# Dilated attention of the sample batches: each key scored once, its multiplicity in the bias, new keys in spare columns

## The reference, cut to what matters

```python
DIL_CONFIGS = ((128, 1), (512, 4), (2048, 16))

def _dilated_sample(q, kv_all, n_buf, slopes):
    outs, lses = [], []
    for win, dil in DIL_CONFIGS:
        j = jnp.arange(win // dil + 1)
        idx = n_buf + jnp.arange(Tn)[:, None] - j[None] * dil
        g = kv_all[:, jnp.maximum(idx, 0)]
        s = jnp.einsum('bqhd,bqjhd->bhqj', q, g[:, :, :, 0]).astype(jnp.float32) * SCALE
        s = s - slopes[:, None, None] * (j * dil).astype(jnp.float32)
        p, lse = _masked_softmax(s, idx >= 0)
        ...
    return _combine_dilations(outs, lses)     # weights: softmax over the three lses
```

## Time and profile before

| what | value |
|---|---|
| median of three runs | 2346.24 us |
| span of the profiled execution (no other time is given for it) | 2350.6 us |
| PE busy | 2262.0 us, 96% of the span |
| DVE, POOL, ACT busy | 891.3, 647.0, 566.5 us |
| mean granted TensorE clock | 0.988 |
| bytes moved | 448.21 MB |
| one sample batch | 39.2 us, 16 of them |

### The profile page before, as it was taken

One profiled execution on the slowest core, in us unless ns is written; L12 is line 12 of the kernel. 1 busy time (PEld: TensorE's weight loads), 2 busy tenths in 40 slices (PEclk: granted clock), 3 DMA queues, 4 the chain that ended last, 5 costly groups with the idle time before them and its releaser, 6 DMA issues.

```text
span 2350.6 us, 43764 instructions
## 1 busy us (share of the span) xinstructions
PE 2262.0 (96%) x13712; PEld 1618.1 (69%) x13712; DVE 891.3 (38%) x2374; ACT 566.5 (24%) x1356; POOL 647.0 (28%) x719
## 2 busy tenths in 40 slices
PE   7999999999999999999999999999999999999998
PEld 4545567676766777777745556667676677777776
DVE  2003764333353222336510147434344522233374
ACT  2111651112122422220111046311111133221202
POOL 0001760101043343344100047410102424343340
PEclk8999999999999999999999999999999999999999
DMA  9643017888864454455375320387888535444441
GB/s 348 218 165 94 6 55 269 294 295 288 301 251 149 167 185 167 167 194 193 115 268 197 134 63 0 133 301 283 306 286 299 211 117 205 179 180 172 167 167 41
DMA packets 128819, 448.21 MB, mean 191 GB/s; under 512 B 17953, under 2 KB 89890, under 8 KB 107554
## 3 DMA queue, kind: packets, MB, share of 16 engines
q1 hardware_dynamic: 118768, 416.45, 48.6%
q10 hardware_dynamic: 9906, 29.98, 3.7%
HBM read 435.76 MB, written 152.57 MB: 250 GB/s over the span
## 4 chain that ended last, share of the span: by engine, by line
PE 89%; issue 4%; DVE 4%; DMA 1%; POOL 1%; ACT 1%; DVEq 0%; SPq 0%; POOLq 0%; ACTq 0%
PE bank L1067 39%; PE bank L1150 14%; PE bank L1363 10%; PE bank L1431 3%; PE bank L1539 3%; PE bank L1298 2%; PE bank L1330 2%; PE bank L1310 2%; PE bank L1163 1%; PE bank L1485 1%; PE bank L1564 1%; POOL zone L919 1%; PE bank L1048 1%; PE bank L1511 1%; PE bank L1541 1%
## 5 line engine op out<-in xcount | busy, mean ns | idle before, releaser
L1067 PE MATMUL bank<-zone,ring 128*128 128x288 f32 x1664 | 426.3, 408 | 9.2 <-DVE zone L1704 6.6
L1067 PEld LDWEIGHTS bank<-zone,ring 128*128 128x128 f32 x1664 | 316.1, 191 | 103.0 <-DVE zone L1704 12.0
L1067 PE MATMUL bank<-zone,w 128*128 128x288 f32 x1408 | 353.5, 406 | 0.0
L1150 PE MATMUL bank<-ring,hT 128*128 128x512 f32 (+2 forms) x800 | 334.5, 572 | 6.8 <-DMA ring<-in_w_in 5.0
L1067 PEld LDWEIGHTS bank<-zone,w 128*128 128x128 f32 x1408 | 267.5, 190 | 73.9
L1150 PEld LDWEIGHTS bank<-ring,hT 128*128 128x128 f32 (+1 forms) x800 | 149.0, 191 | 161.4 <-issue 150.2
L873 POOL TENSOR_TENSOR w<-ring 128x512 f32<-128x512 f32 x72 | 95.6, 1328 | 555.9 <-PE bank L1067 309.4
L1363 PE MATMUL bank<-ring,w 128*128 128x128 f32 x2048 | 242.5, 277 | 0.0
L1363 PEld LDWEIGHTS bank<-ring,w 128*128 128x128 f32 x2048 | 233.0, 192 | 4.1 <-issue 3.8
L611 ACT COPY zone<-bank 128x288 f32<-128x288 f32 x72 | 28.6, 398 | 569.5 <-PE bank L1067 569.5
L986 POOL TENSOR_TENSOR zone<-constants,stat 128x1024 f32<-128x1024 f32 x16 | 30.3, 1896 | 457.2 <-DVE stat L2063 457.2
(11 more groups left out here) (256 smaller groups left out, 2791.2 us busy)
## 6 DMA issues: line engine op xcount, KB each, us to landing
out_dil_s<-in_state_kv_dil SPq DMA_DIRECT2D x48, 2720.0 KB, 12.1
ring<-in_w_units SPq DMA_DIRECT2D x72, 1024.0 KB, 4.8
zone<-in_dilated_v SPq DMA_DIRECT2D x16, 3072.0 KB, 12.7
ring<-in_cache_kv_cmp SPq DMA_DIRECT2D x256, 128.0 KB, 2.2
ring<-in_cache_kv_sel SPq DMA_DIRECT2D x256, 128.0 KB, 6.1
ring<-in_w_in SPq DMA_DIRECT2D x10, 2048.0 KB, 8.6
zone<-in_dilated_k SPq DMA_DIRECT2D x16, 1280.0 KB, 6.0
zone<-in_dilated_k SPq DMA_DIRECT2D x16, 1024.0 KB, 8.1
```

The costliest lines, as they stand in the source:

```text
L1067: last = mm(dst[:, 0:HALF], lhs[:, k, :], rhs(k), start=first and k == 0, stop=(k == 3), skip_group_check=True)
L1150: last = mm(dst, hT[:, k, t * P:t * P + ROWS[t]], ring[:, n % 2, k * CH:k * CH + width], start=start and k == 0, stop=stop and k == KT - 1)
```

## The change

The dilated keys are held once. A key that several of the three sets hold is scored once, and the logarithm of its count is added to its bias. The keys are: the last 128 (tile "last"); the near tiles, now without those 128, which leaves 96 keys in each; and the far tiles, now without the last 512, which leaves 96 keys in each. The 8 new keys of the batch itself sit in 8 free columns of each near tile, which is then 104 wide. The scores of a batch take 128 + 104 + 96 = 328 columns of a bank, not 448. The tile count stays 13.

POOL writes the new keys into the near tiles for each batch once SP's load is there (`new_keys`), and PE waits for POOL in place of the load. The new values come by a small DMA from the output `dil_s`, to which the projections have stored them; the values are loaded by four DMAs and no longer by two. The matmuls L1465 and L1541 are gone, as are DVE's pair for the new keys and the closing minimum. ACT copies the transposed probabilities in three pieces of 128, 104 and 96 rows, and PE waits for each piece before the first tile that uses it.

```diff
+NEAR, FAR = 96, 96
+K_NEAR = NEAR + NS
+AT_NEAR, AT_FAR = P, P + K_NEAR
+KEYS_D = AT_FAR + FAR
...
                 def load_dilated_k(b):
-                    sp.dma_start(kda, of_batch("dilated_k", b)[:, 0:ND_A, :]).then_inc(kda_ld.sem, 16)
-                    sp.dma_start(kdb, of_batch("dilated_k", b)[:, ND_A:ND_A + 4, :]).then_inc(kdb_ld.sem, 16)
+                    keys = i["dilated_k"][L, ds(b, 1)].rearrange("o q p f -> (o q p) f")
+                    sp.dma_start(kda, keys[:, 0:KA]).then_inc(kda_ld.sem, 16)
+                    sp.dma_start(kdb, keys[:, KA:KA + KB]).then_inc(kdb_ld.sem, 16)
...
-                load_dilated_v(0, 0, ND_TILES - 1)
+                load_dilated_v(0)
...
+                    sp.dma_start(vd[:, 0, :], i["dilated_v_last"][L, ds(b, 1)].rearrange("o q p f -> (o q p) f")).then_inc(
+                        vd_ld.sem, 16)
+                    sp.dma_start(vd[0:NEAR, 1:ND_TILES - 1, :], of_batch("dilated_v", b)[:, 0:ND_TILES - 2, :]).then_inc(
+                        vd_ld.sem, 16)
+                    new = o["dil_s"][L, ds(b, 1), PAST - NS:PAST, CH:2 * CH].rearrange("o q r f -> (o q r) f")
+                    sp.dma_start(vd[NEAR:K_NEAR, 1:5, :], new.unsqueeze(1).to_broadcast([NS, 4, CH])).then_inc(vd_ld.sem, 16)
...
-                    copy(ptd[:, 0:3, :].rearrange("p e r -> p (e r)"), B[:, 0:384])
-                    copy(ptd[0:64, 3, :], B[0:64, 384:512]).then_inc(ptk_act.sem, 1)
+                    for e, R in enumerate((P, K_NEAR, FAR)):
+                        copy(ptd[0:R, e, :], B[0:R, e * P:(e + 1) * P]).then_inc(ptk_act.sem, 1)
...
+                def new_keys(it, b):
+                    pool.wait_ge(s_pad.sem, s_pad.at(it, 1))
+                    pool.wait_ge(kda_ld.sem, kda_ld.at(it, 1))
+                    pool.sem_inc(waits_taken_pool, 1)
+                    nc.gpsimd.tensor_copy(kd_near[:, :, :, NEAR:K_NEAR],
+                                          knb[:, :, ds(b * NS, NS)].unsqueeze(1).to_broadcast([P, 4, 4, NS])).then_inc(
+                                              kd_new.sem, 1)
...
-                    pe.wait_ge(kda_ld.sem, kda_ld.at(it, 1))
+                    pe.wait_ge(kd_new.sem, kd_new.at(it, 1))
...
-                    for p in range(4):
-                        mm(S[:, 384:448], strips[:, 0, p * P:(p + 1) * P], knb[:, p, :], start=False, stop=(p == 3),
-                           skip_group_check=True)
...
-                    mm(bank[7][:], ptd[0:64, 3, :], vsm[:, 256:768], start=False, stop=True,
-                       skip_group_check=True).then_inc(od_full.sem, 1)
...
-                    negated(s_d[:, 0:384], B[:, 0:384], const["b_dil"][:], sm[:, 24:25])
-                    step(new_scores(s_d[:, 384:448], B[:, 384:448], const["nb_newd"][:, new], sm[:, 25:26]))
-                    V.tensor_reduce(stat[:, 26:27], sm[:, 24:26], X, ALU.min).then_inc(td_used.sem, 1)
+                    negated(s_d, B[:, 0:KEYS_D], const["b_dil"][:], stat[:, 26:27]).then_inc(td_used.sem, 1)
```

More of the change, by code:

```diff
@@ L275, in build @@
         s_win = part(m + 1216, 576, rows=high)
-        s_d = part(m + 2048, 448)
+        s_d = part(m + 2048, KEYS_D)
         d_own = part(m + 1792, 512)
@@ L280, in build @@
         ptw = part(stg_at + 1024, 5, 64)
-        ptd = part(stg_at + 1344, 4, P)
+        ptd = part(stg_at + 1344, 3, P)
         gb, gm = part(m + 2496, 192, rows=low), part(m + 2048, 192)
@@ L890, in _ @@
                     kind, t = z_kind(n)
-                    if kind not in ("cs", "wg", "vb"):
+                    if kind not in ("cs", "wg", "vb") or n == NZ - 1:
                         continue
@@ L1520, in batch @@
                     B = bank[TD_BANK[TD_PTD]]
-                    for e in range(4):
-                        R = 64 if e == 3 else P
-                        last = tr(B[0:R, e * P:(e + 1) * P], s_d[:, e * P:e * P + R], ident[:])
+                    for e, (a, z) in enumerate(((0, AT_NEAR), (AT_NEAR, AT_FAR), (AT_FAR, KEYS_D))):
+                        last = tr(B[0:z - a, e * P:(e + 1) * P], s_d[:, a:z], ident[:])
                     last.then_inc(td_full.sem, 1)
-                    pe.wait_ge(vd_ld.sem, vd_ld.at(it, 2))
-                    pe.wait_ge(ptk_act.sem, ptk_act.at(it, 3))
-                    pe.sem_inc(waits_taken_pe, 1)
+                    pe.wait_ge(vd_ld.sem, vd_ld.at(it, 4))
                     for j in range(ND_TILES):
+                        if j in (0, 1, ND_A):
+                            pe.wait_ge(ptk_act.sem, ptk_act.at(it, 3 + (0, 1, ND_A).index(j)))
+                            pe.sem_inc(waits_taken_pe, 1)
                         if j == ND_A:
@@ L2206, in laid_out, with turned @@
     put["state_kv_dil"] = dil.reshape(DEPTH, NB, PAST, D)
-    by4 = dil[:, :, PAST - 4 * P:].reshape(DEPTH, NB, P, 4, 2, 8, HD)
-    by16 = dil.reshape(DEPTH, NB, P, 16, 2, 8, HD)[:, :, :, 0:8]
-    tiles = np.concatenate([dil[:, :, PAST - P:, None], by4, by16], 3)
-    put["dilated_v"] = tiles[..., 1, :, :].reshape(DEPTH, NB, P, ND_TILES, CH)
-    put["dilated_k"] = tiles[..., 0, :, :].reshape(DEPTH, NB, P, ND_TILES, 4, 2, HD).transpose(
-        0, 1, 5, 6, 3, 4, 2).reshape(DEPTH, NB, P, ND_TILES, CH)
+    last = dil[:, :, PAST - P:]
+    near = dil[:, :, PAST - WIN:PAST - P].reshape(DEPTH, NB, NEAR, 4, 2, 8, HD)
+    far = dil.reshape(DEPTH, NB, P, 16, 2, 8, HD)[:, :, 0:FAR, 0:8]
+    put["dilated_v_last"] = last[..., 1, :, :].reshape(DEPTH, NB, P, CH)
+    put["dilated_v"] = np.concatenate([near, far], 3)[..., 1, :, :].reshape(DEPTH, NB, NEAR, ND_TILES - 1, CH)
+    def turned(rows, room):
+        k = rows[..., 0, :, :].reshape(DEPTH, NB, rows.shape[2], -1, 4, 2, HD).transpose(0, 1, 5, 6, 3, 4, 2)
+        k = np.pad(k, [(0, 0)] * 6 + [(0, room - rows.shape[2])])
+        return k.reshape(DEPTH, NB, P, -1)
+    put["dilated_k"] = np.concatenate([turned(last[:, :, :, None], P), turned(near, K_NEAR), turned(far, FAR)], -1)
     return {n: np.ascontiguousarray(v) for n, v in put.items()}
```

72 lines of the change are left out of this document (39 added, 33 removed).

## The result

| | before | after |
|---|---|---|
| median (lowest to highest) | 2346.10 us (2341.94 to 2347.63) | 2378.67 us (2367.63 to 2382.45) |
| profiled span | 2350.6 us | 2380.6 us |
| PE busy | 2262.0 us | 2237.0 us |
| mean granted TensorE clock | 0.988 | 0.977 |
| one sample batch | 39.24 us | 41.93 us (mean of 12) |

The change makes the kernel slower: the ratio is 1.0133, 95% interval 1.0104 to 1.0163. The forecast was 2315 us, range 2303 to 2330. It was wrong, in sign too. The profiled execution of the changed kernel (2382.45 us) is the slowest of its four, 4 us above their median.

What follows compares the result with a forecast made beforehand. TensorE, 89% of the chain, was taken to bound the kernel. Terms 0.31 + 0 + 0.22 + 0.49 + 0.97 = 1.99 us a batch, 31.8 over 16, taken as 31, gave 2315 us; own range 2309 to 2321, with A and B 2303 to 2330.

Steps and rivals of the forecast that it cites:

- Narrower tiles: PE's near and far score matmuls: classes 0.16 and 0.22 us shorter; kept 0.31 early and 0.22 late a batch.
- rival A: Score matmul rounds keep 0.11 us because weight loads set them; 1.46 us a batch saved, 2323 us; chance 0.13.
- the floor of 0.10: Score matmuls: by the skill's 25 ns minimum between starts, a round of four could not fall under 0.10 us.
- L1465 gone: Removed matmul before L1475: its 1.04 us becomes waiting for DVE's `gs`, 1.2 us idle in all; kept 0.
- rival D: The clock falls in the new 1.2 us idle time before L1475; 2342 us, no change; chance 0.04.
- C: Rival: all removed PE work counts, 3.19 us a batch, needing `gs` a microsecond earlier; 2295 us; chance 0.06.
- Transposes and copies: Dilated probabilities before L1539: one transpose fewer, and PE starts after ACT's first, 128-column copy; kept 0.49 us a batch.
- L1541 gone: Removed matmul before L1548, 1.05 us: kept 0.97 us a batch, with 0.08 of new idle time.
- rival E: Value matmuls on tiles of 96 and 104 rows lose their overlap; 101 us slower, 2447 us; chance 0.05.
- POOL's new keys: POOL's copy of new keys: hidden, except in a layer's first batch, where 0.4 plus a 0.2 us hop offsets a shorter load.
- the last sentence of the parts: SP's value DMAs, 4 for 2 with 21% fewer bytes: issues covered by its wait for selected outputs, so no time added.
- Rival B: SP sets the pace through late compression pages; PE keeps about 1.0 us a batch, 2330 us; chance 0.07.

Runs made afterwards that it cites:

- e7: e3 with SP issuing the value loads behind the selection's loads and ScalarE issuing the small load of new rows later; 2328.51 us.
- e3: Changed kernel with every value tile padded to 128 rows and loaded on 128 partitions, the small load of new rows moved to ScalarE; 2322.01 us.
- e1: Kernel before with eight value loads on various partition ranges put first, one at a time; rows 0 to 95 took 10.1 us, 0 to 127 took 8.0.
- e10: Changed kernel, loads still on 96 rows, with the small load of new value rows issued by ScalarE and not SP; 2360.28 us.
- e5: Kernel before with loads on differently placed row sets put first, one set at a time; rows 0 to 63 at 171 GB/s, 96 evenly spread at 324.

## Why the prediction was wrong, step by step

The mechanisms on PE, which the prediction worked out at length, came as it said:

- *Narrower tiles:* 1.91 for 2.07 and 0.87 for 1.08; forecast 0.16 and 0.22 less, measured 0.16 and 0.21. The moving columns set a round, not the 32-column load (rival A falls). With 96 columns a round of four starts every 0.083 us, with 128 every 0.109; so the floor of 0.10 that the prediction set beside its sum does not hold here.
- *L1465 gone:* the wait for `gs` is 1.27 (forecast 1.2), DVE named, and the clock stays at full speed behind it (rival D falls, for this gap; C falls too).
- *Transposes and copies:* 0.55 for 0.66, and a wait of 0.45 for 0.81 (forecast 0.5). *L1541 gone:* L1570 follows the last tile with no idle time.
- *Value tiles of 96 and 104 rows* keep their overlap: 16 matmuls in 1.90, as before (rival E falls). POOL's new keys are waited for once a layer, 3.0 us where the load cost 2.74.

With transfers nearly out of the way the sum is seen: e7's period in its profiled execution is 37.34 us, beside a forecast of 37.25. The spans agree with it: e3's 2320.9 less its 6.3 us of waits for pages is 2314.6, and e7's is 2310.9, its fastest, beside a forecast of 2319.6.

The step that failed is the last sentence of the parts: "The value DMAs (4 for 2, 21% fewer bytes) are issued while SP waits for the selected outputs anyway." The issues are indeed covered. But fewer bytes were taken for no more time. On an idle machine rows 0 to 95 take a quarter longer than 128 rows of the same length (e1), and in the kernel the large value load lands after 16.6 us, shown below, where it took 12.7. And the prediction did not ask what a slower load does behind that wait: the 16 selection issues there stretch from 9.80 to 14.06 us, and the page numbers and pages queue up behind them. PE then waits 42.3 us in all for pages and selected rows, and the matmuls behind those waits run slow.

```profile
zone<-in_dilated_v SPq DMA_DIRECT2D x16, 2112.0 KB, 16.6
```

(The page of e10, where the landing is recorded.)

Rival B named that place, and was given 0.07. Its slack was right: 2.3 us in the worst batch, less 1.99 that the change takes. Its price was not. (Its sum is also off: 1.99 less 1.1 - 0.3 leaves 1.2 a batch and not 1.0, so 19 us and 2327, not 2330.) It counted two issues, 1.1 us; the list grew by 4.26 in the selection issues and 0.23 behind them. By B's own sum, 37.25 + 4.26 + 0.23 - 0.3 = 41.4 us a batch; measured 41.93. Its counter-argument, that SP's list has a wait behind these issues, holds for the issues and not for what the slow queue does behind the wait.

## What to carry over

When a change makes a tile narrower, look at which partitions its transfers touch before counting bytes: a load that uses rows 0 to 63 and 64 to 127 unequally can be slower than a full one, and here padding it to 128 rows was worth more than the bytes it added. Take the issuing engine's list as a ring with its own period, and price a slower queue by what it does to every issue behind it, not by the issues you add. And price a new wait of several microseconds on PE with the matmuls after it, which ran at half the clock here: 1.7 us on top of a wait of 3.7.

## What was not expected of the hardware

- Rows 0 to 95, 32 to 127 and 0 to 111 at 214, 212 and 248 GB/s, where 0 to 127 has 355 and rows 32 to 95 have 280 in a load so short that its ends weigh (e1, e5). In the middle of the evenly spread loads a packet of 22,528 bytes took 836 ns, on rows 0 to 63 some 1770.
- Sixteen small DMA issues on SP do not take a fixed time. From one to the next it is 0.57 us for the pages, with no large load queued, 0.49 for the selection's when they come ahead of the values, and 0.94 on the mean behind the slow value loads (14.06 / 15). The mean hides that most stay at 0.38 us each and a few, from the seventh on, take up to 5.58.
- Waits of 1.27 us left the clock at full speed; 3.69 and 4.16 us did not, and the next 8 and 12 matmuls took 3.68 and 2.93 us.
